# Eight recurrent heads: maxima spread one step earlier, denominators squared on ScalarE, other operations on VectorE

## The reference, cut to what matters

```python
w_intra = jnp.exp(d - m_loc[..., None])
w_inter = jnp.exp(inter - m_loc)
sw = jnp.einsum('bhtd,bhsd->bhts', qc, kc) * w_intra
num = w_inter[..., None] * jnp.einsum('bhtd,bhde->bhte', qc, c) + jnp.einsum('bhts,bhse->bhte', sw, vc)
qn = w_inter * jnp.einsum('bhtd,bhd->bht', qc, n) + jnp.sum(sw, axis=-1)
den = jnp.maximum(jnp.abs(qn), jnp.exp(-m_loc))
hc = num / den[..., None]
...
c_new = a[..., None, None] * c + jnp.einsum('bhs,bhsd,bhse->bhde', w, kc, vc)
...
hn = hc * lax.rsqrt(jnp.mean(hc * hc, axis=-1, keepdims=True) + EPS)
hn = hn.reshape(bt, t, A_HV) * g_head.astype(F32)
out = (jax.nn.sigmoid(o.astype(F32)) * hn).astype(h.dtype) @ w_out
```

## Time and profile before

| | |
|---|---|
| Median of 3 runs | 1271.05 us (1270.9 to 1271.4) |
| The profiled execution: time, span | 1270.95 us, 1269.2 us |
| PE busy | 1242.3 us, 98% of the span |
| DVE, ACT, POOL busy | 58%, 46%, 8% |
| Recurrent stage with its eight heads | about 317 to 375 us of the span |

### The profile page before, as it was taken

One profiled execution on the slowest core, in us unless ns is written; L12 is line 12 of the kernel. 1 busy time (PEld: TensorE's weight loads), 2 busy tenths in 40 slices (PEclk: granted clock), 3 DMA queues, 4 the chain that ended last, 5 costly groups with the idle time before them and its releaser, 6 DMA issues.

```text
span 1269.2 us, 22196 instructions
## 1 busy us (share of the span) xinstructions
PE 1242.3 (98%) x8929; PEld 1217.6 (96%) x8929; DVE 737.7 (58%) x1156; ACT 582.5 (46%) x918; POOL 96.2 (8%) x117
## 2 busy tenths in 40 slices
PE   6999999999999999999999999999999999999996
PEld 6999999999889999999999999999996899999996
DVE  7565655565787655554555565654556576565433
ACT  7454533443455554533334554533443465454332
POOL 3000001100323000000000000000020110000011
PEclk9999999999999999999999999999999999999998
DMA  8434244633434444334543744334567743433441
GB/s 303 166 132 165 101 137 153 206 125 124 136 123 148 160 158 139 138 114 159 179 166 133 241 147 151 136 114 144 184 232 287 282 162 133 165 133 123 137 137 41
DMA packets 35994, 200.50 MB, mean 158 GB/s; under 512 B 4362, under 2 KB 6538, under 8 KB 20450
## 3 DMA queue, kind: packets, MB, share of 16 engines
q1 hardware_dynamic: 33858, 192.34, 43.7%
q0 software_dynamic: 2080, 7.39, 1.8%
HBM read 193.14 MB, written 6.57 MB: 157 GB/s over the span
## 4 chain that ended last, share of the span: by engine, by line
PE 92%; DVE 3%; issue 1%; ACT 1%; DMA 1%; SPq 0%; POOL 0%; POOLq 0%; DVEq 0%; ACTq 0%
PE bank L429 30%; PE bank L431 30%; PE bank L430 30%; DMA raw<-vc_in 1%; DVE cn L1495 0%; PE bank L539 0%; ACT junk L1059 0%; DMA raw<-w_in 0%; PE bank L550 0%; DVE dmat L1450 0%; PE bank L489 0%; DVE x L1729 0%; PE bank L761 0%; ACT dmat L1052 0%; DVE w_lo L1244 0%
## 5 line engine op out<-in xcount | busy, mean ns | idle before, releaser
L429 PE MATMUL bank<-h_hi,w_hi 128*128 128x320 f32 x1920 | 597.5, 311 | 11.5 <-DVE h_lo L1256 10.5
L431 PE MATMUL bank<-h_hi,w_lo 128*128 128x320 f32 x1920 | 594.1, 309 | 0.0
L430 PE MATMUL bank<-h_lo,w_hi 128*128 128x320 f32 x1920 | 594.1, 309 | 0.0
L919 ACT ACTIVATE w_hi<-raw 128x1024 fp32r<-128x1024 f32 (+1 forms) x368 | 335.8, 959 | 458.4 <-PE bank L431 454.2
L1244 DVE TENSOR_TENSOR w_lo<-raw,w_hi 128x1024 fp32r<-128x1024 f32 (+1 forms) x368 | 392.9, 1109 | 117.9 <-ACT w_hi L919 117.8
L429 PEld LDWEIGHTS bank<-h_hi,w_hi 128*128 128x128 f32 x1920 | 361.2, 188 | 14.1 <-DVE w_lo L1244 10.4
L430 PEld LDWEIGHTS bank<-h_lo,w_hi 128*128 128x128 f32 x1920 | 361.3, 188 | 0.4
L431 PEld LDWEIGHTS bank<-h_hi,w_lo 128*128 128x128 f32 x1920 | 361.2, 188 | 0.0
L430 PE MATMUL bank<-f_lo,w_hi 128*128 128x320 f32 x704 | 216.5, 308 | 0.0
L429 PE MATMUL bank<-f_hi,w_hi 128*128 128x320 f32 x704 | 216.5, 307 | 0.0
L431 PE MATMUL bank<-f_hi,w_lo 128*128 128x320 f32 x704 | 216.5, 307 | 0.0
(11 more groups left out here) (208 smaller groups left out, 616.5 us busy)
## 6 DMA issues: line engine op xcount, KB each, us to landing
raw<-w_in SPq DMA_DIRECT2D x88, 1024.0 KB, 4.8
raw<-w_out SPq DMA_DIRECT2D x64, 704.0 KB, 4.1
raw<-w_a SPq DMA_DIRECT2D x12, 1024.0 KB, 4.8
raw<-w_kv SPq DMA_DIRECT2D x8, 1024.0 KB, 4.8
raw<-vc_in SPq DMA_DIRECT2D x16, 512.0 KB, 6.4
raw<-kc_in SPq DMA_DIRECT2D x12, 512.0 KB, 4.7
raw<-w_oa SPq DMA_DIRECT2D x4, 1024.0 KB, 5.2
raw<-w_q SPq DMA_DIRECT2D x4, 1024.0 KB, 4.8
```

Of the source, the lines that this page charges most:

```text
L429: pe.matmul(out, wh, mh, start=first, stop=False)
L430: pe.matmul(out, wh, ml, start=False, stop=False)
L431: return pe.matmul(out, wl, mh, start=False, stop=last)
L919: sc.activation(w_hi[:, n_at % 2, part * w:part * w + w], raw[:, raw_of(n_at) % RAW, part * w:part * w + w], ACT.Copy).then_inc(hi_done, 1)
```

## The change

What it does, part by part:

1. PE issues `spread_maxima` one turn earlier: head 1's before the loop, head h + 2's behind `o_chunk(h + 1)` and ahead of `head_turn(h)`. `sel` and `neg_hl` get 128 rows instead of 40.
2. DVE does `decay(h + 1)` and `spread_queries(h + 1)` at the head of the turn, before it waits for head h's outputs. The prompt's first 256 columns of exponents shrink to 128; ACT takes the other 128 straight from bank 4 with a bias. So ACT has three exponentials where it had one, and does them ahead of `head_squares(h)`.
3. The denominators: ACT squares them (128x3); `least` (made once) is compared with the square in one DVE operation. Four small DVE operations become one. The factor 0.5 and the +1 of the gate move into `gated` and into `par`, so `gate_half` goes; `z_split` multiplies by the halved gain.
4. `kwm` moves from POOL to DVE; the copy of the prompt's state moves from DVE to ACT. L655's four matmuls of 64 columns become eight of 32.
5. `z_split` 0 and 1 move ahead of head 7's squares, 2 and 3 ahead of its scaling and states; `head_turn(7)` moves from kt = 2 to kt = 5.

```diff
                 else:
                     pe.wait_ge(qm_done, 2 * h)
+                    pe.wait_ge(w_done, 3 * h)
                 pe.matmul(bank[4][:, 0:384], sel[:, h, :], neg_hl[:, :], start=True, stop=True).then_inc(head_n, 1)
...
+            spread_maxima(1)
             for h in range(H):
                 head_outputs(h)
-                if h + 1 < H:
-                    spread_maxima(h + 1)
                 sample_states(h)
                 if h + 1 < H:
                     if h % 2:
                         scores_of_two(h + 1)
                     o_chunk(h + 1)
+                    if h + 2 < H:
+                        spread_maxima(h + 2)
...
-                if kt == 2:
+                if kt == 5:
                     head_turn(H - 1)
...
             def decay(h):
                 sc.wait_ge(d_done, h + 1)
-                sc.activation(dmat[:, :], dmat[:, :], ACT.Exp).then_inc(w_done, 1)
+                sc.wait_ge(qm_done, 2 * h + 2)
+                sc.activation(dmat[:, 128:256], bank[4][:, 128:256], ACT.Exp, bias=cols[:, 0, h:h + 1]).then_inc(w_done, 1)
+                for part in (slice(0, 128), slice(256, 448)):
+                    sc.activation(dmat[:, part], dmat[:, part], ACT.Exp).then_inc(w_done, 1)
...
                 sc.wait_ge(head_o, h + 1)
-                sc.wait_ge(den_done, h + 1)
+                if h >= 1:
+                    sc.wait_ge(s_in, h)
+                sc.activation(den[:, :].unsqueeze(2),
+                              bank[6][:, 0:3 * (DV + 1)].rearrange("p (t d) -> p t d", t=3)[:, :, DV:DV + 1],
+                              ACT.Square).then_inc(ssq_h, 1)
...
             for h in range(H):
-                head_squares(h)
                 if h + 1 < H:
                     decay(h + 1)
-                    head_scale(h)
                 else:
                     sc.wait_ge(unit_done, U_OA)
                     z_split(0)
                     z_split(1)
-                    head_scale(h)
-                    for g in range(2, H):
+                head_squares(h)
+                if h % 2 == 0:
+                    prompt_state(h)
+                if h + 1 == H:
+                    z_split(2)
+                    z_split(3)
+                head_scale(h)
+                if h + 1 == H:
+                    for g in range(4, H):
                         z_split(g)
...
             for h in range(H):
-                denominators(h)
-                variances(h)
                 if h + 1 < H:
                     decay(h + 1)
                     spread_queries(h + 1)
...
+                ve.wait_ge(head_o, h + 1)
+                if h + 1 < H:
+                    spread_keys(h + 1)
+                if h % 2 == 0:
                     weights(h + 1)
-                    states(h)
+                variances(h)
+                if h % 2 and h + 1 < H:
+                    weights(h + 1)
...
+                states(h)
+                if h + 1 < H:
                     for k, part in HALVES.get(h, ()):
                         split_half(U_A + k, U_A + k, part)
                     keep_gate(h + 1)
                     gated(h)
-                    gate_half(h + 1)
```

More of the change, by code:

```diff
@@ L120, in trunk_program @@
                 cols = sb("cols", [128, 3, 128], f32, own)
+                least = sb("least", [128, 3, H], f32, own)
                 g40 = sb("g40", [40, T], f32, own)
@@ L126, in trunk_program @@
                 neg = sb("neg", [8, 384], f32, own)
-                neg_hl = sb("neg_hl", [40, 384], f32r, own)
+                neg_hl = sb("neg_hl", [128, 384], f32r, own)
                 mt = sb("mt", [8, T], f32, own)
@@ L653, in head_outputs @@
                     for t in range(2):
-                        for g in range(2):
-                            pe.matmul(bank[2][64 * g:64 * g + 64, 0:DV], kw[:, t, (h + g) * 64:(h + g) * 64 + 64],
-                                      v_tok[:, t, h + g, 0:DV], start=(t == 0), stop=(t == 1),
+                        for a in range(4):
+                            pe.matmul(bank[2][32 * a:32 * a + 32, 0:DV], kw[:, t, h * 64 + 32 * a:h * 64 + 32 * a + 32],
+                                      v_tok[:, t, h + a // 2, 0:DV], start=(t == 0), stop=(t == 1),
                                       skip_group_check=True)
@@ L1060, in head_squares, with prompt_state @@
                                   accum_out=ssqh[:, t:t + 1]).then_inc(ssq_h, 1)
+            def prompt_state(h):
+                sc.wait_ge(head_st, h + 1)
+                if h >= 2:
+                    sc.wait_ge(cp_out_s, 16 * (h // 2))
+                sc.activation(cpn[:, :], bank[2][:, 0:DV], ACT.Copy).then_inc(cp_done, 1)
             def head_scale(h):
@@ L1072, in z_split @@
                 sc.wait_ge(z_done, h + 1)
-                sc.activation(h_hi[:, h, :], og[:, h, :], ACT.Copy).then_inc(hh_done, 1)
+                sc.wait_ge(half_gain, 1)
+                sc.activation(h_hi[:, h, :], og[:, h, :], ACT.Copy, scale=par[:, P_HEAD + h:P_HEAD + h + 1]
+                              ).then_inc(hh_done, 1)
             decay(0)
@@ L1330, in first_post @@
                 rms_of(0)
+                ve.tensor_scalar(par[:, P_HEAD:P_HEAD + H], par[:, P_HEAD:P_HEAD + H], 0.5, None, ALU.mult
+                                 ).then_inc(half_gain, 1)
                 ve.wait_ge(s_con, 48)
@@ L1440, in _ @@
             ve.wait_ge(cols_done, 2)
+            chain.link(ve.scalar_tensor_tensor(out=least[:, :, :], in0=cols[:, :, 96:96 + H], scalar=EPS,
+                                               in1=cols[:, :, 96:96 + H], op0=ALU.mult, op1=ALU.mult))
             weigh_keys(0)
@@ L1463, in spread_queries, with spread_keys @@
                         ALU.mult).then_inc(qm_done, 1)
+            def spread_keys(h):
+                if h >= 2:
+                    ve.wait_ge(head_st, h - 1)
+                ve.tensor_tensor(kwm[:, h % 2, :, :],
+                                 kw[0:NS, 2, h * DK:h * DK + DK].unsqueeze(1).to_broadcast([NS, 4, DK]),
+                                 con[0:NS, C_B4:C_B4 + 4].unsqueeze(2).to_broadcast([NS, 4, DK]), ALU.mult
+                                 ).then_inc(kwm_done, 1)
             def weights(h):
                 ve.wait_ge(head_s, h // 2 + 1)
-                ve.wait_ge(w_done, h + 1)
+                ve.wait_ge(w_done, 3 * h + 3)
                 ve.tensor_tensor(pmat[:, 0:448], score_bank[h % 2][:, 0:448], dmat[:, :], ALU.mult).then_inc(p_done, 1)
[L1470 to L1476, removed]
-            def variances(h):
[L1480 to L1485, removed]
+            def variances(h):
+                ve.wait_ge(ssq_h, 4 * h + 4)
+                chain.link(ve.scalar_tensor_tensor(out=den[:, :].unsqueeze(2), in0=den[:, :].unsqueeze(2), scalar=EPS,
+                                                   in1=least[:, :, h:h + 1], op0=ALU.mult, op1=ALU.max))
                 ve.scalar_tensor_tensor(out=var[:, :], in0=ssqh[:, :], scalar=1.0 / DV, in1=den[:, :],
@@ L1520, in _ @@
             split_at(U_A + 9)
+            ve.wait_ge(kw_done, 3)
+            spread_keys(0)
             keep_gate(0)
-            gate_half(0)
             for h in range(H):
-                denominators(h)
-                variances(h)
                 if h + 1 < H:
@@ L1534, in _ @@
                     gated(h)
-                    gate_half(h + 1)
                 else:
[L1537 to L1540, removed]
+                    for g in range(4, H - 1):
                         z_split(g)
```

51 lines of the change are left out of this document (21 added, 30 removed).

## The result

The changed kernel takes 1275.26 us in the median of 8 runs (1274.38 to 1275.68), the kernel before 1271.22 in 8 runs (1270.9 to 1272.04). The ratio is 1.0029, with an interval of 1.002 to 1.0037: slower by 4 us. The profiled execution has a span of 1273.5 us against 1269.2.

What follows compares the result with a forecast made beforehand. PE, 98% busy, bounds the kernel before; the new DVE, ACT and POOL loop would make it wait. The terms 3.8 - 1.0 + 0.35 + 0.85 give +4.0 us, 1275.1 beside the median, range 1271.0 to 1278.0.

Steps and rivals of the forecast that it cites:

- The ring: Closed path through DVE, ACT and POOL, from one DVE weight half to the next: 8.23 us a head, bounds 8.0 and 8.6.
- The Trainium skill's figures: Fixed ScalarE cost per instruction: three exponentials 0.89 us instead of 0.75, time 0.7 us longer, 1275.8.
- The replay: Heads 0 to 6 on PE: waits from head 2 on, 5.5 us in all; head 6's turn at 371.1, +3.8.
- rows of 0.7 to 1.9 at each of five turns: Sign in the trace: PE waits 0.7 to 1.9 us before `head_turn` of heads 2 to 6, released by ACT's `ot`.
- PE's own work: PE's matmuls in the heads: 1.8 us less needed in all, if nothing makes PE wait.
- Behind the heads: Output projection after the heads: -1.0 for a pause gone, +0.35 at kt = 4, +0.85 at the second unit.
- the pause of 1.0: PE's pause ahead of the projection's first chunk goes, as `z_split(0)` no longer waits for head 7's squares: -1.0 us.
- the pause at kt = 4: PE waits for `z_split(4)`, which stands behind `head_scale(7)` on ACT: +0.35 us.
- that at the second unit: PE waits at the second output unit, as its split follows the late `head_turn(7)` at kt = 5: +0.85 us.
- Priced at nothing: `weights`, `states`, `kwm` and the prompt copy on ACT were priced at nothing, as lying beside the ring.
- `weights`, `states`, `kwm` ... stay beside this path: In DVE's idle time of over 1 us before its weight half: no cost; without that cover `kwm` some 0.35 a head.
- The rival that PE stays the bound: The new loop fits under PE, so only PE's terms count: -1.95, 1269.1 us, not slower; chance 0.12.

Runs made afterwards that it cites:

- two order experiments: Changed kernel with ACT's squares put ahead of the three exponentials, 1269.58 us; changed kernel with ACT's weight half put ahead of the scaling, 1269.64 us.
- two copies: Changed kernel plus an unread ACT copy of 128x384, heads 0 to 6: between exponentials and squares 1277.98 us; between squares and scaling 1275.22 us.
- the short ring: Changed kernel with ACT's weight half ahead of the scaling and head 7's turn at kt = 4: 1268.73 us.
- the experiment on PE's part: Kernel before with only the moved maxima (128 rows) and the state matmuls of 32 columns: 1271.75 us, ratio 1.0006.
- made together: Changed kernel with squares ahead of exponentials, ACT's weight half ahead of the scaling, and head 7's turn at kt = 4: 1268.71 us.

## Why the prediction was right

I forecast 1275.1 us with 0.77 for slower; 1275.26 was measured. The mechanism was the forecast one; that the sum came out within 0.2 us is in part luck, since a miss in the heads and one behind them cancel. By its steps:

- **The ring** was the mechanism. The two order experiments and the two copies show it. Forecast 8.23 us a turn, measured 8.12. `decay` took 0.83 and 0.71 in turn (0.75 forecast, its bounds 0.71 and 0.82), the queries to ACT 0.50 (0.43), the three exponentials 334.27 to 334.99 = 0.72 (0.75), the denominator's square 0.05 (0.12), the squares to `den` 0.92 (1.00), `gated` 0.39 (0.47), the scaling 0.77 (0.75). The Trainium skill's figures ("VectorE: DVE Perf Modes", the TRN2 errata) had made the exponentials 0.89. One by one they are recorded as 0.37 and 0.55 for two, 0.92 in all, which is near that estimate; but each starts before the record of the one ahead ends, and it is the 0.72 from start to start that the ring pays.
- **The replay**: head 6's turn +3.8 forecast, +3.36 measured. Turn 0 came at 323.91 instead of 323.6, and the change has no part in that: ahead of head 0's maxima PE was already 0.33 late (308.64 against 308.31 before), from there to the next matmul of the gate it took 1.73 us against 1.72, so the 0.1 that I gave those maxima was nothing, and the kernel with the turn at kt = 4, whose lists are the same up to there, has this turn at 323.61. Head 1's `ot` was complete at 330.02 all the same (330.0 forecast), as `gated(0)` to `var` took 3.47 (324.50 to 327.97) where I had added up 3.72. From there the shorter ring made the rest (5 x 0.11 = 0.55). The pauses are 4.1 us in PE's rows against 5.5. Each costs more than its row says: from `spread_maxima` to the turn it is 0.18 us without a pause (323.73 to 323.91) and 0.59 with one of 0.26 (337.66 to 338.25), 0.15 on top. Five times that makes 4.9. As a sign I had given rows of 0.7 to 1.9 at each of five turns; three of the five (0.26, 0.57 and 0.56) are under it.
- **PE's own work**: the maxima at 0.18 us (0.175 forecast), L646 to L666 0.77 (0.80). Head 1's turn to head 6's is 39.50; less 4.9 it is 34.6, against 34.8 forecast.
- **Behind the heads**: the pause of 1.0 went, as forecast; the pause at kt = 4 is 0.36 in its row (0.35), that at the second unit 0.73 (0.85). The second unit starts 3.90 later than before (385.28 against 381.38), where the sum said 4.0, but its parts differ: the first chunk is 2.34 later (2.8 forecast), and from there to the second unit 1.56 are lost (1.20), more than the two rows hold. The span has 0.4 more, which is the difference of the DMA waits at L835 and stood in no term of the forecast. That the turn at kt = 5 is too late was half the story in this kernel: with the turn at kt = 4 DVE's queue holds `gated(7)` instead. With the short ring the earlier turn alone took the pause away.
- **Priced at nothing**: that the keys move to VectorE. The step "`weights`, `states`, `kwm` ... stay beside this path" holds for the 0.42 us that they take there, and the sum took the half at 1.13 from a turn where GpSimd's operation lay elsewhere, so the forecast was not hurt. But nothing is the wrong price for the move: left on GpSimd, the keys stretch this ring by 1.5 us over five turns. The kernel before has the like: `gate_half` (L1370) took 0.77 us beside GpSimd's operation (340.14 to 340.77), and 0.33 a turn earlier, at 332.65, just behind one that ended at 332.62. I had read the 0.77 as `gate_half` with the tanh ahead of it; it is the record of `gate_half` alone.

The change shortens DVE's list and PE's own work, but what it takes off is less than what its order puts on the ring (7.49 us a turn before, 8.12 after). The rival that PE stays the bound was wrong by the ring alone: where the experiments bring it under PE's pace, the time is 1269.6, near that rival's 1269.1.

## What to carry to other kernels

When the bound engine is 98% busy, look at the closed ring of the others: take one instruction's start, and follow who releases whom until the same instruction of the next turn; an edit costs or gives what it changes in that sum, until the ring is as fast as the bound engine. Work that can run while the ring waits for a slow helper (here POOL's power, 0.9 us) belongs there, and not behind the helper's answer. Where two such edits give the same time, as here, the ring is likely below the bound; made together they gave no more than one.

## What the runs showed of the hardware

- A GpSimd operation of 0.63 us (64x256, two SBUF inputs) lengthened a VectorE operation of 1.23 us beside it to 1.93; with 0.42 us shared, to 1.51. In other turns of the same kernel the VectorE operation took 1.28 and the GpSimd one 1.54.
- Of eight like loads that GpSimd issued (stored state, in the experiment on PE's part), one landed 7.2 us after its issue, where their median is 3.3. In the changed kernel the slowest took 3.8.
- A pause of TensorE cost about 0.15 us beyond the idle time in its row (0.41 for a row of 0.26, 0.72 for one of 0.57). The row counts from the end of the last record, and without a pause the next matmul starts 0.15 before that end (L605 is recorded at 0.33 us and the next starts 0.18 after it).
- Consecutive ScalarE operations overlap in their records: 0.92 us of three exponentials in 0.72, and a square of 128x3 recorded at 0.16 us delays the next by 0.05.
